# One query slot computed head by head, the first exponentials taken earlier, and four row batches mixed one step sooner in a two-layer PEER kernel

## The chip, the cores and the metric

The kernel runs on one core of a Trainium2 chip. The metric is the device time of one execution in microseconds (us); smaller is better. TensorE (PE) multiplies, ScalarE (ACT) and VectorE (DVE) work on vectors, GpSimd (POOL) issues the gathers of table rows, and SyncE (SP) issues the loads of weights.

## What is computed

The program runs two transformer layers and then a hybrid mixer and a mixture of experts. The change touches one part of each of the two layers, the PEER feed-forward:

```python
def peer_ffn(h, w_q, sub_keys, u_tab, v_tab):     # T = 256 tokens, 8 heads
    q = (xt @ w_q).reshape(T, PEER_HEADS, 2, PEER_HALF)
    s = jnp.einsum('thpd,hpnd->thpn', q, sub_keys)          # 16 blocks of 128 scores
    sv, si = lax.top_k(s, 16)
    cand = sv[:, :, 0, :, None] + sv[:, :, 1, None, :]
    cv, ci = lax.top_k(cand.reshape(T, PEER_HEADS, 256), 16)
    eidx = i1 * PEER_NKEYS + i2                             # 16 rows for a token and head
    gates = softmax(cv)
    ...
    act = gelu(einsum('cd,ckd->ck', xc, u_tab[ic]))
    return einsum('ck,ckd->cd', gc * act, v_tab[ic])
```

All of it is float32.

## The kernel before

The 256 tokens are two tiles of 128. A pair is one head of one tile, so there are 16 pairs, and each picks 16 rows for every token: 256 "rows" in a layer. One row here is one gather of 128 table rows of 2048 words (u and v side by side), 1 MB. `PICKS` is 256, and pairs 0 to 7 belong to tile 0.

The query matrix comes in four slots of 2 MB, with two heads (four blocks) each. `ring` holds two slots. SP loads a slot when the one two places before it has been used, which it sees by the semaphore `tile_done`; behind the four query slots it loads two slots of the gate matrix in the same way, and, when slot 3 is done, `proj_w` and `pT` (1 MB and 0.25 MB).

- Slot 0 (`first_heads`) is computed for tile 0, all four blocks, then for tile 1: query matmuls (L582), small matmuls that turn two pieces of a conditioning vector each (L528), and the score matmuls with the keys (L592). ACT takes each result out of PSUM (L1085, L1087).
- Slots 1 to 3 (`features`, L463, for both tiles at once, in four groups of matmuls j = 0 to 3) give queries that ACT evicts (L1092). Then come the score matmuls (L613) and their evictions (L1102).
- DVE's `topk(p)` finds the rows of pair p: its last instruction (L1538) releases `rows_ready`, and POOL then issues 16 gathers (L2010). The gathers have `ROWS` = 12 buffers, so gather n waits until row n - 12 has been mixed (`v_done`).
- DVE's loop over pairs takes the dot product of each row with the token (L1598). Between the dots it does one step of `topk(p + 2)`; the first step of `topk(2)` stands behind the dot of row 0 and waits for the scores of slot 1.
- For each batch of four rows ACT's `batch(at)` computes the gelu (L1074), DVE the gate (L1609), and ACT four diagonal matrices (L1080). PE's `mix_rows` (L566) then multiplies each diagonal with the v half of the row, adds into PSUM and releases `v_done`.
- `exponents(p)` (L1067) are the softmax exponentials of pair p. DVE's loop can't begin pair p without them.

PE works in program order. Between the query slots it mixes batch 0 halfway through slot 2, batch 4 behind slot 2's scores, and batch 8 halfway through slot 3; from row 12 on it mixes behind slot 3. ACT's order is written out by hand too: `exponents(0)` behind the second eviction of slot 1, `batch(0)` and `batch(4)` behind the first of slot 2, `batch(8)` behind the scores of slot 2, `batch(12)` behind the first eviction of slot 3.

Of the kernel before, what the change touches and what calls it, by code (L numbers as in the profile page):

```python
# [14 lines left out]
P = 128  # L15
T = 256
TT = T // P
# [4 lines left out]
PH = 8  # L22
# [12 lines left out]
PICKS = PAIRS * TOPK  # L35
BATCH = 4
# [7 lines left out]
    ("a_x", 2, "AA"), ("a_gates", 1, "A" * 8), ("a_y", 2, "AA"), ("a_out", 2, "DD"),  # L44
    ("peer_q0", 4, "AAAA"),
    ("ple_gate0", 2, "A"),
    ("qkv", 6, "AA"), ("bo", 2, "DD"),
    ("peer_q1", 4, "AAAA"),
    ("ple_gate1", 2, "A"),
    ("mix_in", 7, ("AA", "DD", "AA", "AA", "AA", "AA", "DD")), ("mix_out", 2, "DD"),  # L50
)
MIX = (4, 3, 5, 1, 0, 2, 6)
GATES = (0, 1, 2, 4, 5, 6, 3, 7)
CAP = 64
# [57 lines left out]
def build(nc, d):  # L112
# [7 lines left out]
    with ExitStack() as ctx:  # L120
# [321 lines left out]
        def _(pe):  # L442
# [111 lines left out]
            def peer(l, i):  # L554
# [16 lines left out]
                def first_heads():  # L571

                    n = FIRST[f"peer_q{l}"]
                    w = slot_in(n).rearrange("p (k f) -> p k f", k=KC)
                    m = ENDS[n] - 4
                    turn(i, h)
                    for t in range(TT):
                        pe.wait_ge(xT_ready, 4 * i + 4 * l + 2 * t + 2)
                        bank_free(m + 2 * t)
                        for f in range(4):  # L580
                            for k in range(KC):
                                mm = pe.matmul(psum[:, (m + 2 * t) % 3, f * P:(f + 1) * P], w[:, k, f * P:(f + 1) * P],  # L582
                                               xT[:, k, t * P:(t + 1) * P], start=(k == 0), stop=(k == KC - 1))
                        mm.then_inc(tile_done, 1)
                        for s in range(2 * t, 2 * t + 2):
                            turn_condition(8 * l + s)
                        if t == 0:
                            pe.wait_ge(keys_loaded, 16 * (l + 1))
                        pe.wait_ge(act_took, TILE_NTH[m + 2 * t])
                        bank_free(m + 2 * t + 1)  # L590
                        for f in range(4):
                            mm = pe.matmul(psum[:, (m + 2 * t + 1) % 3, f * P:(f + 1) * P], qT[:, f, t * P:(t + 1) * P],  # L592
                                           keys[:, f * NK:(f + 1) * NK], start=True, stop=True)
                        mm.then_inc(tile_done, 1)
# [6 lines left out]

                def half_way(at):
                    return lambda j: mix_early(at) if j == 1 else None

                for s in range(1, 4):
                    features(f"peer_q{l}", s, xT, between=half_way(8 * s - 16) if s >= 2 else None)
# [27 lines left out]

                for n in range(3 * BATCH, PICKS):
                    if n == 148:
# [369 lines left out]
        def _(act):  # L1006
# [54 lines left out]
            def peer(l, i):  # L1061
# [21 lines left out]
                m = tile0(f"peer_q{l}")  # L1083
                for t in range(TT):
                    act.activation(qT[:, 0:4, t * P:(t + 1) * P], tile_in(m + 2 * t).rearrange("p (a b) -> p a b", a=4),  # L1085
                                   ACT.Copy).then_inc(act_took, 1)
                    act.activation(scores[:, t, 0:4, :], tile_in(m + 2 * t + 1).rearrange("p (a b) -> p a b", a=4),  # L1087
                                   ACT.Copy).then_inc(act_took, 1)
                for s in range(1, 4):
                    m = tile0(f"peer_q{l}") + 4 * s  # L1090
# [220 lines left out]
        def _(dve):  # L1311
# [165 lines left out]
            def peer(l, i):  # L1477
# [19 lines left out]
                def topk(p):  # L1497

                    m = tile0(f"peer_q{l}") + 4 * (p % PH // 2)
                    dve.wait_ge(act_took, TILE_NTH[m + 2 + p // PH if p % PH // 2 else m + 1 + 2 * (p // PH)])  # L1500
                    for half in range(2):
# [592 lines left out]
```

## Time and profile before

| | us |
|---|---|
| median of 3 runs | 2948.27 |
| lowest and highest | 2947.35 and 2952.21 |
| the profiled execution | 2960.54 |
| its span, first to last instruction | 2958.7 |
| PE busy, share of the span | 89% |
| DVE, ACT, POOL busy | 46%, 21%, 17% |
| read from memory | 1047.69 MB |

The span is what the profile's time axis covers; 1.8 us of the profiled execution lie around it. That execution took 12.3 us more than the median of the runs without a profile. Times in the text count from the first instruction. A float32 matmul shows as two records, so four mixed rows (eight matmuls) are 16 records. The PEER part of layer 0 runs from about 108 to 822 us, that of layer 1 from about 995 to 1710 us.

### The profile page before, as it was taken

How to read it: one execution, taken by the hardware profiler on the slowest of the kernel's cores; microseconds unless marked ns; L12 is line 12 of the kernel's file. 1: busy time of each engine (PE TensorE's matmuls, PEld its weight loads, DVE VectorE, ACT ScalarE, POOL GpSimd, SP SyncE). 2: the span in 40 equal slices, each digit the busy share in tenths (PEclk: the TensorE clock that was granted, in tenths of full speed). 3: DMA queues.
4: the chain of work that ended last, by engine and by line, in shares of the span. 5: the costliest groups of instructions: out<-in, count | busy, mean ns of one | idle time of the engine just before them, and what ended most of it. 6: DMA issues, size and time to landing. Idle time of an engine off the chain costs nothing.

```text
span 2958.7 us, 28660 instructions
## 1 busy us (share of the span) xinstructions
PE 2623.4 (89%) x9706; PEld 1223.0 (41%) x9706; DVE 1368.7 (46%) x3391; ACT 616.2 (21%) x1232; POOL 489.4 (17%) x526
## 2 busy tenths in 40 slices
PE   8998787887799998787888799889999999999998
PEld 7663333333366663333333366543333232333333
DVE  5657777776425656777776541431111111111111
ACT  3022212232115122222232120211111111111111
POOL 0124333333200124333333200000000000000000
PEclk9999999999999999999999999889999999999999
DMA  5699999999863699999999833447999999899997
GB/s 217 264 377 422 421 421 421 421 420 421 347 240 143 249 377 422 421 421 421 421 421 421 345 127 114 180 199 321 422 422 422 422 422 422 352 422 422 376 400 295
DMA packets 145293, 1049.90 MB, mean 355 GB/s; under 512 B 16272, under 2 KB 16528, under 8 KB 17968
## 3 DMA queue, kind: packets, MB, share of 16 engines
q0 software_dynamic: 74064, 537.56, 43.8%
q1 hardware_dynamic: 70560, 509.12, 42.2%
q10 hardware_dynamic: 576, 2.13, 0.2%
q8 instruction: 41, 0.67, 0.1%
q14 instruction: 52, 0.43, 0.0%
HBM read 1047.69 MB, written 1.05 MB: 354 GB/s over the span
## 4 chain that ended last, share of the span: by engine, by line
PE 54%; DMA 37%; DVE 4%; ACT 2%; issue 1%; another core or an unknown queue 1%; DVEq 1%; SPq 0%; POOLq 0%
PE psum L566 14%; DMA big<-in_moe 13%; DMA uv_more<-in_peer_uv,rows_of 13%; DMA big<-in_peer_uv,rows_of 11%; PE psum L971 11%; PE psum L463 7%; PE psum L997 5%; PE psum L478 5%; PE psum L883 1%; PE psum L952 1%; PE psum L665 1%; PE psum L582 1%; DVE big L1598 1%; DVE uv_more L1598 1%; PE psum L965 1%
## 5 line engine op out<-in xcount | busy, mean ns | idle before, releaser
L566 PE MATMUL psum<-big,gdiag 128*128 128x512 f32 x1880 | 912.7, 642 | 233.1 <-ACT gdiag L1080 233.1
L1598 DVE CUSTOM_DVE_ANT_0 big<-psum,big 128x1024 f32<-128x1024 f32 x470 | 574.4, 1224 | 281.4 <-DMA big<-in_peer_uv,rows_of 274.8
L566 PEld LDWEIGHTS psum<-big,gdiag 128*128 128x128 f32 x1880 | 375.6, 205 | 761.9 <-issue 440.8
L2010 POOL DMA_INDIRECT big<-in_peer_uv,rows_of x470 | 444.7, 946 | 1158.2 <-PE psum L566 779.5
L971 PE MATMUL psum<-big 128*64 128x512 f32 x2240 | 500.9, 596 | 24.4 <-POOLq L2032 23.9
L1976 DVE TENSOR_SCALAR big<-psum 128x512 f32<-128x512 f32 x35 | 24.2, 692 | 667.5 <-PE psum L971 667.5
L971 PEld LDWEIGHTS psum<-big 128*64 128x64 f32 x2240 | 152.8, 137 | 370.7 <-issue 275.1
L997 PE MATMUL psum<-ring,big 128*64 128x512 f32 x1120 | 248.1, 594 | 3.8
L463 PE MATMUL psum<-big,ring 128*128 128x256 f32 x1088 | 241.2, 381 | 0.8 <-DVE big L1362 0.8
L463 PEld LDWEIGHTS psum<-big,ring 128*128 128x128 f32 x1088 | 206.5, 191 | 33.2 <-issue 3.8
L1074 ACT ACTIVATE gelu<-dots,rstd 128x4 f32<-128x4 f32 x128 | 38.0, 297 | 869.1 <-DVE dots L1598 869.1
L1080 ACT ACTIVATE gdiag<-small,gated 128x128 f32<-128x128 f32 x512 | 163.6, 390 | 49.8 <-DVE gated L1609 49.2
L478 PE MATMUL psum<-ring,big 128*128 128x512 f32 x352 | 156.3, 602 | 2.7 <-DVE big L1439 1.4
L997 PEld LDWEIGHTS psum<-ring,big 128*64 128x64 f32 x1120 | 92.5, 137 | 136.8 <-issue 132.1
L1294 ACT ACTIVATE big<-big 128x512 f32<-128x512 f32 x35 | 22.0, 630 | 489.3 <-DVE big L1976 489.3
L478 PEld LDWEIGHTS psum<-ring,big 128*128 128x128 f32 x352 | 66.8, 192 | 84.6 <-issue 79.7
L566 PE MATMUL psum<-uv_more,gdiag 128*128 128x512 f32 x168 | 78.9, 592 | 0.0
L952 PE MATMUL psum<-big 64*128 64x512 f32 x288 | 71.5, 615 | 0.7 <-ACT big L1302 0.7
L883 PE MATMUL psum<-big 128*64 128x512 f32 x288 | 71.3, 617 | 0.0
L1302 ACT ACTIVATE big<-psum 128x512 f32<-128x512 f32 x35 | 20.9, 597 | 231.0 <-PE psum L997 231.0
L1609 DVE SCALAR_TENSOR_TENSOR gated<-gelu,gsum,gexp 128x4 f32<-128x4 f32 x128 | 28.1, 219 | 81.7 <-ACT gelu L1074 79.2
L1598 DVE CUSTOM_DVE_ANT_0 uv_more<-psum,uv_more 128x1024 f32<-128x1024 f32 x42 | 51.4, 1224 | 24.8 <-DMA uv_more<-in_peer_uv,rows_of 24.2
(385 smaller groups left out, 1969.2 us busy)
## 6 DMA issues: line engine op xcount, KB each, us to landing
big<-in_moe SPq DMA_DIRECT2D x256, 1024.0 KB, 20.7
ring<-in_moe SPq DMA_DIRECT2D x128, 1024.0 KB, 19.4
big<-in_ada SPq DMA_DIRECT2D x24, 1024.0 KB, 11.8
ring<-in_peer_wq SPq DMA_DIRECT2D x16, 1024.0 KB
ring<-in_mix_in SPq DMA_DIRECT2D x14, 1024.0 KB
ring<-in_a_in SPq DMA_DIRECT2D x8, 1024.0 KB
ring<-in_ple_gate SPq DMA_DIRECT2D x8, 1024.0 KB
ring<-in_kv SPq DMA_DIRECT2D x8, 1024.0 KB
```

What stands on the lines that cost most here:

```text
L463: mm = pe.matmul(psum[:, (m + t) % 3, f * T:(f + 1) * T], w[:, k, c:c + P], rhs[:, k, :], start=(k == 0), stop=(k == KC - 1))
L478: mm = pe.matmul(psum[:, (m + t) % 3, :], lhs[:, k, t * P:(t + 1) * P], w[:, k, :], start=(k == 0), stop=(k == KC - 1))
L566: mm = pe.matmul(psum[:, OUT_BANK[t] + c, :], gdiag[:, n % DIAGS, :], uv[(PICKS * l + n) % ROWS][:, D + c * 512:D + (c + 1) * 512], start= ...
L582: mm = pe.matmul(psum[:, (m + 2 * t) % 3, f * P:(f + 1) * P], w[:, k, f * P:(f + 1) * P], xT[:, k, t * P:(t + 1) * P], start=(k == 0), sto ...
L883: mm = pe.matmul(psum[CAP * c:CAP * (c + 1), 2, :], S[:, t, :], hs[:, t, c * 512:(c + 1) * 512], start=(t == 0), stop=(t == TT - 1), skip_ ...
L952: mm = pe.matmul(psum[:, 4 + 2 * t + c, :], SGT[r, t * P:(t + 1) * P], Y[r, :], start=False, stop=stop, skip_group_check=True)
L971: mm = pe.matmul(psum[CAP * c:CAP * (c + 1), b, :], xgT[:, k % 4, k // 4, :], wring[k][:, (2 * b + c) * 512:(2 * b + c + 1) * 512], start= ...
L997: mm = pe.matmul(psum[CAP * c:CAP * (c + 1), 2, :], actT[:, j, f * CAP:(f + 1) * CAP], wring[8 + j][:, (2 * f + c) * 512:(2 * f + c + 1) * ...
L1074: act.activation(gelu[:, cols], dots[:, cols], ACT.Gelu_apprx_tanh, scale=rstd[:, t:t + 1]).then_inc(gelu_ready, 1)
L1080: act.activation(gdiag[:, n % DIAGS, :], ident, ACT.Copy, scale=gated[:, n:n + 1]).then_inc(gdiag_ready, 1)
L1598: j = dve.tensor_tensor_reduce(out=u, in0=x, in1=u, scale=1.0, scalar=0.0, op0=ALU.mult, op1=ALU.add, accum_out=dots[:, n:n + 1])
L2010: pool.indirect_dma_start(uv[g % ROWS], None, table, bass.IndirectOffsetOnAxis(rows_of[:, n:n + 1], 0)).then_inc(uv_loaded[g % ROWS], 16)
```

## The change

Three parts. (1) Slot 0 is computed in three parts instead of two: head 0 of tile 0, head 1 of tile 0, then both heads of tile 1 (`FIRST_HEADS`), each with its own queries, evictions and scores; `topk(0)` and `topk(1)` wait for their own head's scores alone. The four turns of the conditioning vector are spread as one, one, two. (2) ACT takes `exponents(0)` right behind the evictions of slot 0, and `batch(0)` behind slot 1's scores and `exponents(1)`. (3) PE mixes batch 0 behind the first group of slot 2 (of four), batch 4 behind its third, batch 8 behind slot 2's scores, and batch 12 halfway through slot 3; behind slot 3 it goes on with row 16.

```diff
-    ("peer_q0", 4, "AAAA"),
+    ("peer_q0", 4, ("AAAAAA", "AAAA", "AAAA", "AAAA")),
...
+FIRST_HEADS = ((0, (0, 1)), (0, (2, 3)), (1, (0, 1, 2, 3)))
...
-                    for t in range(TT):
+                    for part, (t, blocks) in enumerate(FIRST_HEADS):
                         pe.wait_ge(xT_ready, 4 * i + 4 * l + 2 * t + 2)
-                        bank_free(m + 2 * t)
-                        for f in range(4):
+                        q, s = m + 2 * part, m + 2 * part + 1
+                        bank_free(q)
+                        for j, f in enumerate(blocks):
...
-                        for s in range(2 * t, 2 * t + 2):
-                            turn_condition(8 * l + s)
+                        for c in ((0,), (1,), (2, 3))[part]:
+                            turn_condition(8 * l + c)
...
-                def half_way(at):
-                    return lambda j: mix_early(at) if j == 1 else None
+                inside = {2: {0: 0, 2: BATCH}, 3: {1: 3 * BATCH}}
+
+                def mix_inside(s):
+                    return lambda j: mix_early(inside[s][j]) if j in inside[s] else None
...
                     if s == 2:
-                        mix_early(BATCH)
+                        mix_early(2 * BATCH)
...
-                for n in range(3 * BATCH, PICKS):
+                for n in range(4 * BATCH, PICKS):
...
+                exponents(0)
                 for s in range(1, 4):
...
-                        if s == 1 and g == 1:
-                            exponents(0)
                         if s == 2 and g == 0:
-                            batch(0)
                             batch(4)
...
                     if s == 1:
                         exponents(1)
+                        batch(0)
...
-                    dve.wait_ge(act_took, TILE_NTH[m + 2 + p // PH if p % PH // 2 else m + 1 + 2 * (p // PH)])
+                    dve.wait_ge(act_took, TILE_NTH[m + 2 + p // PH if p % PH >= 2 else
+                                                   tile0(f"peer_q{l}") + (5 if p >= PH else 1 + 2 * p)])
```

On ACT, this stands before the change from the first eviction of slot 1 on (`gdiag` are the diagonals, `gexp` the exponentials):

```order
L1092 ACTIVATE big<-psum 128x512 [waits tile_done] x2
L1067 ACT_TABLE_LOAD
L1067 ACTIVATE gexp<-gexp,rstd 128x16 [waits gexp_in]
L1102 ACTIVATE big<-psum 128x512 [waits tile_done] x2
L1067 ACTIVATE gexp<-gexp,rstd 128x16 [waits gexp_in]
L1092 ACTIVATE big<-psum 128x512 [waits tile_done]
L1074 ACT_TABLE_LOAD
L1074 ACTIVATE gelu<-dots,rstd 128x4 [waits dots_ready]
L1080 ACTIVATE gdiag<-small,gated 128x128 [waits gated_act]
L1080 ACTIVATE gdiag<-small,gated 128x128 x3
```

And this stands there after it, from the last eviction of slot 0 on:

```order
L1093 ACTIVATE big<-psum 128x512 [waits tile_done]
L1071 ACT_TABLE_LOAD
L1071 ACTIVATE gexp<-gexp,rstd 128x16 [waits gexp_in]
L1100 ACTIVATE big<-psum 128x512 [waits tile_done] x2
L1107 ACTIVATE big<-psum 128x512 [waits tile_done] x2
L1071 ACTIVATE gexp<-gexp,rstd 128x16 [waits gexp_in]
L1078 ACT_TABLE_LOAD
L1078 ACTIVATE gelu<-dots,rstd 128x4 [waits dots_ready]
L1084 ACTIVATE gdiag<-small,gated 128x128 [waits gated_act]
L1084 ACTIVATE gdiag<-small,gated 128x128 x3
L1100 ACTIVATE big<-psum 128x512 [waits tile_done]
```

The first exponential has moved ahead of slot 1's evictions, and the first gelu with its diagonals ahead of slot 2's first eviction; the number of table loads is the same.

On PE, slot 2 begins like this before the change (L463 is the slot's queries, L566 the mixing of a row, two matmuls each):

```order
L463 MATMUL psum<-big,ring 128x256 [waits act_took,half_loaded3,half_loaded2]
L463 MATMUL psum<-big,ring 128x256 x15
L566 MATMUL psum<-big,gdiag 128x512 [waits gdiag_ready]
L566 MATMUL psum<-big,gdiag 128x512
L566 MATMUL psum<-big,gdiag 128x512 [waits gdiag_ready]
L566 MATMUL psum<-big,gdiag 128x512
L566 MATMUL psum<-big,gdiag 128x512 [waits gdiag_ready]
L566 MATMUL psum<-big,gdiag 128x512
L566 MATMUL psum<-big,gdiag 128x512 [waits gdiag_ready]
L566 MATMUL psum<-big,gdiag 128x512
L463 MATMUL psum<-big,ring 128x256 [waits act_took]
L463 MATMUL psum<-big,ring 128x256 x15
```

And like this after it:

```order
L464 MATMUL psum<-big,ring 128x256 [waits act_took,half_loaded3,half_loaded2]
L464 MATMUL psum<-big,ring 128x256 x7
L567 MATMUL psum<-big,gdiag 128x512 [waits gdiag_ready]
L567 MATMUL psum<-big,gdiag 128x512
L567 MATMUL psum<-big,gdiag 128x512 [waits gdiag_ready]
L567 MATMUL psum<-big,gdiag 128x512
L567 MATMUL psum<-big,gdiag 128x512 [waits gdiag_ready]
L567 MATMUL psum<-big,gdiag 128x512
L567 MATMUL psum<-big,gdiag 128x512 [waits gdiag_ready]
L567 MATMUL psum<-big,gdiag 128x512
L464 MATMUL psum<-big,ring 128x256 x8
L464 MATMUL psum<-big,ring 128x256 [waits act_took]
```

Batch 0 stands eight matmuls earlier in slot 2. Batch 4, formerly behind slot 2's scores, follows eight matmuls before the slot's last ones, and so on for the next two.

## Rows read from the trace of the kernel before

**Rows 1.** The page: memory traffic in 40 equal slices, and the chain by engine.

```profile
GB/s 217 264 377 422 421 421 421 421 420 421 347 240 143 249 377 422 421 421 421 421 421 421 345 127 114 180 199 321 422 422 422 422 422 422 352 422 422 376 400 295
...
PE 54%; DMA 37%; DVE 4%; ACT 2%; issue 1%; another core or an unknown queue 1%; DVEq 1%; SPq 0%; POOLq 0%
```

**Rows 2.** Windows: PE, PEld, DVE, ACT, POOL busy, granted clock, DMA share, GB/s.

```profile
130.00:215.00 85.00, 75.06 (x304) 55.23 (x303) 45.27 (x141) 18.62 (x40) 22.88 (x24) 0.94 0.94 375
215.00:800.00 585.00, 475.62 (x998) 197.84 (x996) 410.78 (x1030) 138.78 (x340) 219.28 (x232) 0.93 1.01 421
1018.00:1105.00 87.00, 77.21 (x306) 55.91 (x305) 46.21 (x143) 20.61 (x44) 23.50 (x25) 0.94 0.94 378
1105.00:1300.00 195.00, 154.75 (x321) 63.86 (x320) 138.98 (x361) 44.44 (x111) 75.76 (x80) 0.93 1.01 422
```

**Rows 3.** The same view, two windows in which the DMA traffic begins.

```profile
130.00:135.00 5.00, 5.00 (x27) 4.46 (x26) 4.33 (x22) 0.31 (x1) 2.88 (x3) 1.00 0.85 288
...
1015.00:1020.00 5.00, 5.00 (x37) 4.77 (x37) 4.19 (x18) 0.74 (x2) 0.94 (x1) 1.00 0.32 72
```

**Rows 4.** Timeline of DVE, layer 0: start us, us, what, [idle before it <- releaser].

```profile
113.33 5.70 DVE L1451 SCALAR_TENSOR_TENSOR big<-big,cond 128x512 f32<-128x512 f32 x7
120.51 0.29 DVE L1487 MAX8 sv<-big 128x8 f32<-128x128 f32 x1 [1.47 <-ACT big L1087]
...
130.39 0.18 DVE L1538 SCALAR_TENSOR_TENSOR rows_of<-picked 128x16 uint32<-128x16 f32 x1
```

**Rows 5.** Timelines of the issuing engines SP and POOL, layer 0.

```profile
213.19 0.43 SPq L384 DMA_DIRECT2D big<-in_ple_proj  x1
...
131.52 1.14 POOL L2010 DMA_INDIRECT big<-in_peer_uv,rows_of  x1 [131.07 <-DVE rows_of L1538]
...
145.57 0.94 POOL L2010 DMA_INDIRECT uv_more<-in_peer_uv,rows_of  x1 [0.31 <-issue]
```

**Rows 6.** Timeline of PE, layer 0.

```profile
130.38 13.98 PE L463 MATMUL psum<-big,ring 128*128 128x256 f32 x64
149.26 3.78 PE L613 MATMUL psum<-keys,big 128*128 128x128 f32 x16 [4.90 <-ACT big L1092]
152.84 7.73 PE L463 MATMUL psum<-big,ring 128*128 128x256 f32 x32
163.55 8.83 PE L566 MATMUL psum<-big,gdiag 128*128 128x512 f32 x16 [2.99 <-ACT gdiag L1080]
...
181.86 7.03 PE L566 MATMUL psum<-big,gdiag 128*128 128x512 f32 x16
...
210.26 2.05 PE L613 MATMUL psum<-keys,big 128*128 128x128 f32 x16 [0.69 <-ACT big L1092]
```

**Rows 7.** Timeline of ACT, layer 0.

```profile
148.61 0.60 ACT L1092 ACTIVATE big<-psum 128x512 f32<-128x512 f32 x1 [10.52 <-remote]
...
151.37 0.60 ACT L1102 ACTIVATE big<-psum 128x512 f32<-128x512 f32 x1 [0.55 <-PE psum L613]
...
195.84 0.60 ACT L1092 ACTIVATE big<-psum 128x512 f32<-128x512 f32 x1 [11.43 <-PE psum L463]
...
196.91 1.28 ACT L1080 ACTIVATE gdiag<-small,gated 128x128 f32<-128x128 f32 x4 [0.29 <-DVE gated L1609]
```

**Rows 8.** Timeline of DVE, layer 0: first step of topk(2), dot of row 3.

```profile
152.39 0.29 DVE L1487 MAX8 sv<-big 128x8 f32<-128x128 f32 x1
...
157.49 1.23 DVE L1598 CUSTOM_DVE_ANT_0 big<-psum,big 128x1024 f32<-128x1024 f32 x1
```

**Rows 9.** Timelines of PE and ACT, layer 1.

```profile
1050.96 8.83 PE L566 MATMUL psum<-big,gdiag 128*128 128x512 f32 x16 [2.99 <-ACT gdiag L1080]
...
1099.76 0.60 ACT L1102 ACTIVATE big<-psum 128x512 f32<-128x512 f32 x1 [0.30 <-PE psum L613]
1100.37 1.28 ACT L1067 ACT_TABLE_LOAD   x1
...
1103.88 1.28 ACT L1080 ACTIVATE gdiag<-small,gated 128x128 f32<-128x128 f32 x4 [0.29 <-DVE gated L1609]
```

More of the change, by code:

```diff
@@ L44 @@
     ("a_x", 2, "AA"), ("a_gates", 1, "A" * 8), ("a_y", 2, "AA"), ("a_out", 2, "DD"),
-    ("peer_q0", 4, "AAAA"),
+    ("peer_q0", 4, ("AAAAAA", "AAAA", "AAAA", "AAAA")),
     ("ple_gate0", 2, "A"),
     ("qkv", 6, "AA"), ("bo", 2, "DD"),
-    ("peer_q1", 4, "AAAA"),
+    ("peer_q1", 4, ("AAAAAA", "AAAA", "AAAA", "AAAA")),
     ("ple_gate1", 2, "A"),
@@ L574, in first_heads @@
                     w = slot_in(n).rearrange("p (k f) -> p k f", k=KC)
-                    m = ENDS[n] - 4
+                    m = ENDS[n] - 6
                     turn(i, h)
-                    for t in range(TT):
+                    for part, (t, blocks) in enumerate(FIRST_HEADS):
                         pe.wait_ge(xT_ready, 4 * i + 4 * l + 2 * t + 2)
-                        bank_free(m + 2 * t)
-                        for f in range(4):
+                        q, s = m + 2 * part, m + 2 * part + 1
+                        bank_free(q)
+                        for j, f in enumerate(blocks):
                             for k in range(KC):
-                                mm = pe.matmul(psum[:, (m + 2 * t) % 3, f * P:(f + 1) * P], w[:, k, f * P:(f + 1) * P],
+                                mm = pe.matmul(psum[:, q % 3, j * P:(j + 1) * P], w[:, k, f * P:(f + 1) * P],
                                                xT[:, k, t * P:(t + 1) * P], start=(k == 0), stop=(k == KC - 1))
                         mm.then_inc(tile_done, 1)
-                        for s in range(2 * t, 2 * t + 2):
-                            turn_condition(8 * l + s)
-                        if t == 0:
+                        for c in ((0,), (1,), (2, 3))[part]:
+                            turn_condition(8 * l + c)
+                        if part == 0:
                             pe.wait_ge(keys_loaded, 16 * (l + 1))
[L589 to L592, printed above, removed]
+                        pe.wait_ge(act_took, TILE_NTH[q])
+                        bank_free(s)
+                        for j, f in enumerate(blocks):
+                            mm = pe.matmul(psum[:, s % 3, j * P:(j + 1) * P], qT[:, f, t * P:(t + 1) * P],
                                            keys[:, f * NK:(f + 1) * NK], start=True, stop=True)
@@ L600, in mix_early @@
                         mix_rows(n)
-                def half_way(at):
-                    return lambda j: mix_early(at) if j == 1 else None
+                inside = {2: {0: 0, 2: BATCH}, 3: {1: 3 * BATCH}}
+                def mix_inside(s):
+                    return lambda j: mix_early(inside[s][j]) if j in inside[s] else None
                 for s in range(1, 4):
-                    features(f"peer_q{l}", s, xT, between=half_way(8 * s - 16) if s >= 2 else None)
+                    features(f"peer_q{l}", s, xT, between=mix_inside(s) if s in inside else None)
                     m = ENDS[FIRST[f"peer_q{l}"] + s] - 2
@@ L1083, in peer @@
                 m = tile0(f"peer_q{l}")
-                for t in range(TT):
-                    act.activation(qT[:, 0:4, t * P:(t + 1) * P], tile_in(m + 2 * t).rearrange("p (a b) -> p a b", a=4),
+                for part, (t, blocks) in enumerate(FIRST_HEADS):
+                    f, n = slice(blocks[0], blocks[-1] + 1), len(blocks)
+                    act.activation(qT[:, f, t * P:(t + 1) * P],
+                                   tile_in(m + 2 * part)[:, 0:n * P].rearrange("p (a b) -> p a b", a=n),
                                    ACT.Copy).then_inc(act_took, 1)
-                    act.activation(scores[:, t, 0:4, :], tile_in(m + 2 * t + 1).rearrange("p (a b) -> p a b", a=4),
+                    act.activation(scores[:, t, f, :],
+                                   tile_in(m + 2 * part + 1)[:, 0:n * P].rearrange("p (a b) -> p a b", a=n),
                                    ACT.Copy).then_inc(act_took, 1)
+                exponents(0)
                 for s in range(1, 4):
-                    m = tile0(f"peer_q{l}") + 4 * s
+                    m = tile0(f"peer_q{l}") + 4 * s + 2
                     for g in range(2):
@@ L1497, in topk @@
                 def topk(p):
-                    m = tile0(f"peer_q{l}") + 4 * (p % PH // 2)
-                    dve.wait_ge(act_took, TILE_NTH[m + 2 + p // PH if p % PH // 2 else m + 1 + 2 * (p // PH)])
+                    m = tile0(f"peer_q{l}") + 4 * (p % PH // 2) + 2
+                    dve.wait_ge(act_took, TILE_NTH[m + 2 + p // PH if p % PH >= 2 else
+                                                   tile0(f"peer_q{l}") + (5 if p >= PH else 1 + 2 * p)])
                     for half in range(2):
```

## The prediction

> **What bounds the kernel now.** I began with the page. Its traffic row stands at 420 to 422 GB/s for most of two stretches, slices 4 to 10 and 16 to 22: these are the gathers of the two PEER parts, and the chain gives DMA 37% of the span [rows 1]. So I cut windows. From 215 to 800 us the DMA engines carry 421 GB/s, from 1105 to 1300 us 422 [rows 2]: there nothing but the amount of data counts. The stretch ahead of each is where time can be had: 375 GB/s from 130 to 215 us and 378 from 1018 to 1105 us [rows 2]. Against 421 that is 85 x (1 - 375/421) = 9.3 us and 87 x (1 - 378/421) = 8.9 us of empty DMA. Part of it is the ramp: 288 GB/s in 130 to 135 us means data from 131.6 us on, and 72 GB/s in 1015 to 1020 us data from 1019.1 us on [rows 3]. What is left, 7.7 and 7.8 us, is starvation in the query slots, and it is all that the change can win there. A layer's gathers end when the DMA has moved all its bytes, so a us of starvation saved or added is a us of the kernel, in each layer. One row is 1.049 MB, at 421 GB/s 2.49 us.
>
> **Part 1, slot 0 by heads.** It removes and adds no matmul: 32 + 32 query matmuls become 16 + 16 + 32. PE should reach slot 1 at the same 130.4 us [rows 6]; the eviction between queries and scores stays behind the turn of the conditioning vector. ACT has two evictions more in a layer, in idle time. `topk(0)` began at 120.51 us after DVE had waited 1.47 us for its scores; before that DVE was busy with the sums until 113.33 + 5.70 = 119.03 us [rows 4]. Head 0's scores have 32 records of 128 columns less ahead of them; 64 records of 256 columns take 13.98 us [rows 6], so these are 3.5 us, and the scores come at 117 us at the latest. DVE is now the limit, and `topk(0)`, with its first rows at 130.39 us [rows 4] and POOL's first gather at 131.52 us [rows 5], comes 1.45 us earlier. I price these 1.45 us at nothing: data flow from 131.6 us already, hardly after POOL's first issue, because SP has issued the weights of slot 2 when slot 0 was done. Earlier gathers change the order of bytes that are moved without a gap: rows 0 to 15 and slots 2 and 3 are 20 rows' worth, enough until 131.6 + 20 x 2.49 = 181.4 us.
>
> The Trainium skill (DMA: Bandwidth & Descriptors, Queues, rings and completion order) says that a DMA engine goes round between the queues that have work, packet by packet. By that the gathers would only take a share of slot 2's bandwidth sooner, which is again nothing in the sum.
>
> **Part 2, exponentials and batch 0.** DVE's loop no longer waits for `exponents(0)`, so the dot of row 0 can be taken sooner, by about the 10.5 us that ACT stood still ahead of 148.61 us [rows 7]. But behind it stands the first step of `topk(2)`, which waits for slot 1's scores, evicted at 151.37 + 0.60 = 151.97 us [rows 7]. That step began at 152.39 us [rows 8]. It gains 0.4 us, and the dot of row 3, which ended at 157.49 + 1.23 = 158.7 us [rows 8], ends at 158.3 us. The gain lies behind that: ACT has no eviction ahead of the gelu any more. From the start of an eviction to the start of the diagonals are 196.91 - 195.84 = 1.07 us, of which 0.5 is the eviction, and the first of four diagonals takes 0.32 us [rows 7]. So the first diagonal is ready at about 159.3 us. Before, batch 0 began on PE at 163.55 us after a wait of 2.99 us [rows 6].
>
> **Part 3, the mixing in the slots.** In slot 2 the first group of queries ends at about 156.9 us, about half of the 32 records that took 7.73 us from 152.84 us on [rows 6]. PE then waits 2.4 us for the diagonal instead of 2.99. Batch 4 needs nothing new. Batch 8 now stands right behind slot 2's scores, but its gelu stands on ACT behind the evictions of these scores; batch 12 stands right behind the half slot whose eviction ACT takes before that gelu. Either time PE waits for eviction, gelu, gate and first diagonal: 1.07 + 0.32 = 1.4 us from the eviction's start [rows 7], 1.45 with the semaphore. Before the change, batches 4 and 8 found their diagonals ready (181.86 us follows the scores without a wait [rows 6]).
>
> What this does to the DMA is a balance of two things. Four rows more are mixed ahead of slot 3's end, so four gathers more, 4 x 2.49 = 9.96 us of data, are to be had before the last weights come. And slot 3 ends later, with the loads behind it (second gate slot, projection), issued 0.9 us after its scores (210.26 + 2.05 = 212.31, and 213.19 us [rows 5, 6]). It ends later by 6.87 us for four rows (7.03 us of records that overlap [rows 6]), plus 2 x 1.45 us for the new waits, less 0.6 us for the shorter one: 9.2 us. So the starvation falls by 0.8 us only. If the stretch at half clock does not come again that made batch 0 take 8.83 us where batch 4 took 7.03 [rows 6, 9], slot 3 ends 1.8 us less late, 7.4 us, and 2.6 us are saved. I take the middle, 1.7 us, since the wait ahead of batch 0 is only a little shorter than the one that had it. The granted clock's mean was 0.94 in both stretches [rows 2]. The same rows hold in layer 1, where batch 0 waited 2.99 us and took 8.83 us too [rows 9].
>
> The Trainium skill (TensorE: Matmul & The Clock Gate, Part 1) says that the array's usual state is the throttled one and that only activity releases it. Taken as it stands it speaks against the change, which adds two gaps; with batch 0 slow as before, its sum is 0.8 us a layer and 2946.7 us.
>
> **Behind slot 3** PE now meets row 16 at once, and row 16's gelu waits for the scores' evictions, a table load, an exponential and another table load. In layer 1 the second eviction began at 1099.76 us and the diagonals at 1103.88 us [rows 9], so the first is ready 4.5 us after the scores, and row 28 can be gathered 1.8 us later, 6.3 us after the scores. Gate slot, `proj_w` and `pT` are 3.25 rows' worth, 8.1 us of data from an issue at 0.9 us: work until 9.0 us in these terms. The new stall on PE is covered by 2.7 us, less if gathers take longer from issue to data than weights; without cover it costs its own length.
>
> **Sum.** The profiled execution (2960.54 us, of which 2958.7 are span) would lose 2 x 1.7 = 3.4 us. It stands 12.3 us over the median of the runs, and I carry the difference over: 2948.3 - 3.4 = 2945 us. Below 0.2%, 5.9 us, a measurement of this kernel can't tell a change from none.
>
> **Rivals.** *The pause behind slot 1 shortens.* PE's last record of slot 1 ends at 144.36 us, yet ACT is released at 148.61 us by something that the view calls remote [rows 6, 7]; that is 2.1 us after POOL's last issue of the first twelve ends at 146.51 us [rows 5]. PE then ran its scores in 3.78 us instead of 2.05, and 32 records of slot 2 in 7.73 instead of 13.98 / 2 = 7.0 us [rows 6]. I can't name the cause. If it is tied to POOL's train, which now ends 1.45 us sooner, slot 3 ends 1.5 to 2 us sooner: 3 to 4 us more, 2941 us. If it goes, 4.25 us with the 1.7 and 0.7 us of slow matmuls go, more than the 6.0 us of starvation left in each layer: 2933 us. Chance 0.25 for both, mostly the first.
>
> *The timed runs have no such pause.* Their 12.3 us less than the profiled one speak for it. Then slot 3 ended at about 205.6 us before (212.31 less 4.25, 1.7 and 0.7), 30 rows' worth of data (24 rows, slots 2 and 3 and a gate slot) lasted to 131.6 + 74.7 = 206.3 us, and there was hardly any starvation to save. The new slot 3 ends 6.87 + 2.9 + 0.5 = 10.3 us later against 9.96 us of data: 0.3 to 1 us slower in each layer, 2949 us. Chance 0.2.
>
> *The earlier start counts in full.* 2 x 1.45 us more: 2942 us. It would need an empty DMA until POOL's gathers come, and [rows 3] speak against it. Chance 0.05.
>
> *Slower: half clock in the slots.* If the two new waits each bring a stretch at half clock like that behind the 2.99 us wait, 1.8 us each, slot 3 ends 9.2 + 3.6 = 12.8 us later against 9.96 us of data: 2.8 us lost in each layer, 2954 us. It decides from 9.96 us of delay on, and from 12.9 us on it is slower by 0.2%. That the 0.69 us waits at the scores bring nothing speaks against it; that the new ones are twice as long, for it. Chance 0.12.
>
> **How the numbers follow.** My forecast, 0.8 to 2.6 us saved in each layer with a us or two of slack either way, 2942 to 2948 us, has 0.38. Faster by over 0.2% means under 2942.4: most of the first rival, half of the third, and a tail of the forecast, 0.27. Slower means over 2954.2: half of the fourth and what I have not seen, 0.13. The rest, 0.60, is no difference. The range from 2937 to 2954 us leaves out 0.2: the case in which the pause goes, and what lies beyond the slow clock.
>
> **What would show it.** `topk(0)` starts at about 119.05 us with no wait for ACT; the first gather at about 130.1 us, with the data's start unmoved. The dot of row 0 comes near 141 us and that of row 1 only behind 152 us. Batch 0 is mixed from about 159.4 us, with waits of some 1.4 us ahead of batches 8 and 12. Slot 3's scores end at 219.7 to 221.5 us, row 16 starts 4.5 us later. The traffic has no gap any more behind 181.4 us, its last one has moved from before 213 us to before 222 us, and 130 to 215 us carry more than 375 GB/s. The forecast is wrong if slot 3 ends outside these limits, if ACT's pause at 138 to 148.6 us changes, or if a gap opens behind row 28.

## The result

The changed kernel takes 2955.55 us (median of 22 runs), the kernel before 2947.93 us (22 runs beside it): ratio 1.0022, interval 1.0012 to 1.0031. The change costs 7.6 us. Two later comparisons give 1.0019 (1.0006 to 1.0033) and 1.0023 (1.0011 to 1.0035). The profiled execution of the changed kernel spans 2953.1 us.

The page of the changed kernel, traffic and chain, beside [rows 1]:

```profile
GB/s 217 254 402 406 421 421 421 421 421 422 353 229 141 246 410 414 421 422 421 421 422 421 345 127 116 179 198 328 422 422 422 421 422 422 350 422 422 379 401 295
...
PE 55%; DMA 35%; DVE 5%; ACT 2%; issue 1%; DVEq 1%; SPq 0%; POOLq 0%
```

Slices 3 and 15 carry more than before (402 for 377, 410 for 377), slices 4 and 16 less (406 for 422, 414 for 421). The gap has not gone, it has moved behind 215 us. The windows of the changed kernel (columns as in [rows 2]), first the four stretches of [rows 2], then the end of slot 3 in layer 0 piece by piece and that part of either layer as a whole:

```profile
130.00:215.00 85.00, 76.60 (x298) 53.20 (x298) 45.55 (x142) 15.00 (x34) 26.45 (x28) 0.96 0.98 401
215.00:800.00 585.00, 475.98 (x1020) 200.48 (x1018) 410.25 (x1030) 142.57 (x345) 214.18 (x228) 0.93 1.01 417
1018.00:1105.00 87.00, 77.90 (x312) 54.85 (x311) 44.91 (x139) 15.66 (x36) 26.30 (x28) 0.98 0.99 409
1105.00:1300.00 195.00, 155.90 (x336) 65.29 (x334) 142.09 (x371) 49.88 (x120) 74.09 (x79) 0.93 1.00 414
...
215.00:220.00 5.00, 4.31 (x27) 3.68 (x26) 0.00 (x0) 1.18 (x2) 0.00 (x0) 1.00 0.78 324
220.00:225.00 5.00, 1.48 (x12) 1.06 (x10) 0.83 (x2) 4.35 (x8) 0.00 (x0) 0.87 0.73 244
225.00:230.00 5.00, 5.00 (x6) 2.05 (x7) 4.63 (x12) 0.71 (x3) 0.94 (x1) 0.50 0.99 417
230.00:235.00 5.00, 5.00 (x12) 2.23 (x11) 4.67 (x16) 1.57 (x5) 1.87 (x2) 0.95 0.93 317
235.00:240.00 5.00, 5.00 (x13) 2.28 (x12) 4.69 (x11) 0.00 (x0) 2.81 (x3) 1.00 1.01 375
205.00:245.00 40.00, 35.80 (x110) 19.66 (x109) 25.37 (x67) 9.39 (x21) 12.17 (x13) 0.91 0.93 357
1075.00:1135.00 60.00, 53.55 (x168) 30.07 (x167) 33.43 (x92) 14.94 (x35) 18.45 (x20) 0.97 0.98 397
```

There are two gaps, one ahead of the gate weights (324 and 244 GB/s) and one behind row 28's gather (317 and 375 GB/s); another 1.0 us is missing between 205 and 215 us (378 and 382 GB/s). Against 421 GB/s the last two rows are 40 x (1 - 357/421) = 6.1 us and 60 x (1 - 397/421) = 3.4 us of empty DMA.

PE in layer 0 (start us, us, what, [idle before it]):

```profile
132.24 13.98 PE L464 MATMUL psum<-big,ring 128*128 128x256 f32 x64
146.90 2.05 PE L617 MATMUL psum<-keys,big 128*128 128x128 f32 x16 [0.69 <-ACT big L1100]
148.79 3.62 PE L464 MATMUL psum<-big,ring 128*128 128x256 f32 x16
156.32 10.05 PE L567 MATMUL psum<-big,gdiag 128*128 128x512 f32 x16 [3.91 <-ACT gdiag L1084]
...
187.90 5.42 PE L567 MATMUL psum<-big,gdiag 128*128 128x512 f32 x12 [1.56 <-ACT gdiag L1084]
...
203.50 7.13 PE L567 MATMUL psum<-big,gdiag 128*128 128x512 f32 x16 [1.56 <-ACT gdiag L1084]
...
218.23 2.05 PE L617 MATMUL psum<-keys,big 128*128 128x128 f32 x16 [0.69 <-ACT big L1100]
...
224.89 15.05 PE L567 MATMUL psum<-big,gdiag 128*128 128x512 f32 x28 [2.83 <-ACT gdiag L1084]
```

The reader is to see four waits for diagonals, and behind two of them mixing that is slow: 10.05 us for 16 records that take 7.03 us at the full clock, and 15.05 us for 28 that take 12.2 us. The window 225 to 230 us shows the granted clock at 0.50, the lower of the two levels (1.2 GHz), and the one behind the first wait 0.54:

```profile
155.00:160.00 5.00, 3.68 (x5) 1.61 (x6) 4.67 (x17) 1.58 (x5) 0.00 (x0) 0.54 1.01 423
```

DVE, POOL and ACT of the same execution, their timelines one after the other:

```profile
120.82 0.28 DVE L1493 MAX8 sv<-big 128x8 f32<-128x128 f32 x1
...
130.69 0.18 DVE L1545 SCALAR_TENSOR_TENSOR rows_of<-picked 128x16 uint32<-128x16 f32 x1
...
132.70 1.14 POOL L2017 DMA_INDIRECT big<-in_peer_uv,rows_of  x1 [132.25 <-PE psum L559]
...
210.91 0.94 POOL L2017 DMA_INDIRECT big<-in_peer_uv,rows_of  x1 [0.78 <-PE psum L567]
228.94 0.94 POOL L2017 DMA_INDIRECT big<-in_peer_uv,rows_of  x1 [17.09 <-PE psum L567]
...
146.25 0.60 ACT L1100 ACTIVATE big<-psum 128x512 f32<-128x512 f32 x1 [6.31 <-PE psum L464]
...
155.11 0.30 ACT L1078 ACTIVATE gelu<-dots,rstd 128x4 f32<-128x4 f32 x1 [4.02 <-DVE dots L1605]
```

`topk(0)` no longer waits for ACT, and its rows come 1.6 us sooner, counted from the start of slot 0's queries (130.69 - 111.61 = 19.1 us for 130.39 - 109.75 = 20.6 us before). But POOL's first gather is released by PE (the conditioning vector, L559), not by DVE. POOL stands still for 17.09 us from row 27 to row 28. And ACT's eviction at 146.25 us follows PE at once: the pause of [rows 7] is not in this execution.

### The profile page after: what moved, and what is told of

It reads as the page before. It is cut to its first block, busy times and chain, and to the rows that moved or that the text cites. A ratio compares the mean times of both kernels' runs of the same rounds, so it can differ in the third digit from the quotient of the medians.

```text
span 2953.1 us, 28668 instructions
## 1 busy us (share of the span) xinstructions
PE 2624.6 (89%) x9706; PEld 1220.8 (41%) x9706; DVE 1367.5 (46%) x3391; ACT 616.7 (21%) x1236; POOL 486.5 (16%) x526
## 4 chain that ended last, share of the span: by engine, by line
PE 55%; DMA 35%; DVE 5%; ACT 2%; issue 1%; DVEq 1%; SPq 0%; POOLq 0%
PE psum L567 15%; DMA big<-in_moe 13%; DMA big<-in_peer_uv,rows_of 12%; PE psum L975 11%; DMA uv_more<-in_peer_uv,rows_of 10%; PE psum L464 7%; PE psum L1001 5%; PE psum L479 5%; PE psum L887 1%; DVE big L1605 1%; PE psum L956 1%; PE psum L669 1%; PE psum L584 1%; PE psum L969 1%; PE psum L629 1%
```

## The experiments

Sixteen runs in four series of four; a series shares its runs of the kernel before. Times are medians with the ratio to the kernel before, timed beside it, and its 95% interval. "Slot 3" below is the start of its scores, less the start of slot 0's queries, since that start lies at 109.3 to 109.8 us in some executions and at 111.3 to 112.0 us in others, whatever the kernel.

### The kernel before again, and the parts

**e1_before_again**, the kernel before unchanged.

> The kernel before, unchanged. Theory A (the pause of 4.2 us behind slot 1 belongs to that one profiled execution, and the timed runs have none): ratio 1.000, and a new profile may come without the pause; then its span is about 2946 us instead of 2958.7, slot 3's scores end some 6.5 us earlier than 212.3 us and 130 to 215 us carry about 400 GB/s. Rival B (the pause is a part of this program): it stands there again in both layers, with a span near 2958.7 us.

Measured: 2948.01 us, 1.0002 (0.999 to 1.0015), span 2941.8 us. Its profile has no pause.

**e2_early_exp**, parts 1 and 2 with the order of mixing of before:

```diff
-inside = {2: {0: 0, 2: BATCH}, 3: {1: 3 * BATCH}}
+inside = {2: {1: 0}, 3: {1: 2 * BATCH}}
...
-                        mix_early(2 * BATCH)
+                        mix_early(BATCH)
...
-                for n in range(4 * BATCH, PICKS):
+                for n in range(3 * BATCH, PICKS):
```

> Parts 1 and 2 of the change (slot 0 by heads, exponents(0) and batch(0) early on ACT) with the mixing order of the kernel before. Theory A (the loss comes from the mixing order, which ends slot 3 later and exposes row 16): no loss, 0 to 3 us faster than before (ratio 0.999 to 1.000), slot 3's scores end at or before the time they end without a pause, about 205 us. Rival C (the loss comes from the heads or from the early exponentials): it stays slower, ratio near 1.002.

Measured: 2946.68 us, 0.9996 (0.9987 to 1.0005). Batch 0 waits 0.46 us and takes 7.13 us; slot 3 is 89.7 us; 205 to 245 and 1075 to 1135 us both carry 421 GB/s, so the DMA is full where it was empty for 1.3 us in each layer of e1. It is not full further on in layer 0. The same window of e2 and of e1, in that order:

```profile
560.00:610.00 50.00, 49.04 (x115) 21.55 (x114) 35.06 (x93) 17.28 (x35) 18.88 (x21) 1.00 0.99 399
560.00:610.00 50.00, 47.71 (x112) 20.83 (x111) 36.17 (x98) 17.28 (x35) 18.53 (x20) 1.00 1.01 421
```

That is 50 x (1 - 399/421) = 2.6 us of empty DMA, as much as the two layers have gained.

**e3_no_heads**, parts 2 and 3 with slot 0 as before (`peer_q0` and `peer_q1` "AAAA", the two-tile loop in slot 0):

> Parts 2 and 3 of the change (early exponentials and batch 0, mixing one step sooner) with slot 0 as before. Theory A: as slow as the change, ratio 1.002 to 1.003. Rival C1 (the loss comes from slot 0 by heads): as fast as before, 1.000.

Measured: 2954.33 us, 1.0021 (1.001 to 1.0032); slot 3 106.7 us. Without part 1 the loss is the same.

**e4_three_batches**, the change with twelve rows ahead of slot 3's end:

```diff
-inside = {2: {0: 0, 2: BATCH}, 3: {1: 3 * BATCH}}
+inside = {2: {0: 0, 2: BATCH}, 3: {1: 2 * BATCH}}
...
-                    if s == 2:
-                        mix_early(2 * BATCH)
...
-                for n in range(4 * BATCH, PICKS):
+                for n in range(3 * BATCH, PICKS):
```

> The change, but only three batches are mixed ahead of slot 3's end as in the kernel before: batch 0 and batch 4 inside slot 2 as in the change, batch 8 halfway through slot 3, nothing behind slot 2's scores, and row 12 first behind slot 3. Theory A: slot 3's scores end 8 to 9 us earlier than in the change (220.3 us less 111.61 - 109.75 for the later start of layer 0's part), the DMA traffic has no gap behind row 28, and the loss is gone: ratio 0.999 to 1.001. Rival C (heads or early exponentials): near 1.002.

Measured: 2953.17 us, 1.0012 (1.0002 to 1.0023). PE in layer 0 and the two windows of this kernel:

```profile
156.06 10.11 PE L567 MATMUL psum<-big,gdiag 128*128 128x512 f32 x16 [3.91 <-ACT gdiag L1082]
...
207.50 2.05 PE L617 MATMUL psum<-keys,big 128*128 128x128 f32 x16 [0.69 <-ACT big L1098]
```

```profile
205.00:245.00 40.00, 35.13 (x102) 17.15 (x101) 23.03 (x58) 12.55 (x28) 15.45 (x16) 0.99 0.95 388
1075.00:1135.00 60.00, 53.95 (x160) 28.71 (x159) 35.70 (x99) 15.90 (x35) 20.82 (x22) 0.97 0.97 399
```

It mixes as many rows ahead of slot 3's end as the kernel before, batches 0 and 4 eight matmuls earlier, and has slot 3 at 96.2 us for 94.0: the early mixing alone delays slot 3 by 2.2 us, and more of the DMA is empty (3.1 + 3.1 us) than in e16 below. The expected 0.999 to 1.001, no loss without the four rows, was missed: part of the loss is there without them. What the four rows do by themselves is seen in e14 below.

### Undoing one piece of part 3

**e5_row16_early** and **e6_batch0_later** each undo one, **e7_later_and_row16** both, **e8_heads_only** is part 1 alone. The edit of e5, on ACT, in slot 3 and in the loop behind it:

```diff
                         if s == 3 and g == 0:
                             batch(12)
+                            exponents(2)
+                            batch(16)
...
-                        if at >= 16:
+                        if at >= 20:
                             batch(at)
...
-                    if p + 2 < PAIRS:
+                    if 0 < p < PAIRS - 2:
                         exponents(p + 2)
```

The edit of e6, on PE (batch 0 where it was, batches 4 and 8 behind slot 2's scores):

```diff
-inside = {2: {0: 0, 2: BATCH}, 3: {1: 3 * BATCH}}
+inside = {2: {1: 0}, 3: {1: 3 * BATCH}}
...
                     if s == 2:
+                        mix_early(BATCH)
                         mix_early(2 * BATCH)
```

> The changed kernel with one move: the exponential of the third pair and the gelu and diagonals of rows 16 to 19 stand on ACT right behind batch 12, ahead of the evictions of slot 3's second group of queries and of its scores. Theory (two gaps: slot 3 ends too late, and row 16's stall of 2.83 us with half clock behind it makes row 28's gather late): PE's row 16 follows the scores of slot 3 with no wait and at the full clock, the traffic between 230 and 240 us rises from 317 and 375 GB/s to 420, which is 1.8 us, and in layer 1 about 0.9 us; the gap before 225 us stays. Time 2.7 us under the change, ratio to the kernel before 1.0013. Rival one (the whole loss is slot 3's late end): the ratio stays at 1.0022. Rival two (the exponential or the dots of rows 16 to 19 are not ready in slot 3, ACT waits for DVE and slot 3's scores come later still): slower than the change, 1.003.

> The changed kernel with batch 0 mixed where the kernel before mixes it, between the two groups of slot 2, and batches 4 and 8 both behind slot 2's scores; batch 12 halfway slot 3, so still 16 rows ahead of slot 3's end. Theory (it is the waits and the half clock of the early batch 0, not the number of rows): PE waits about 0.5 us ahead of batch 0 and takes 7.1 us for it, the 1.56 us wait ahead of batch 8 goes, slot 3's scores come near 210 us instead of 218.2, which is less than four rows' 9.96 us of data behind the 203.4 us of the kernel before, so the gap before 225 us goes; ratio 1.0000 to 1.0005. Rival (the number of rows mixed ahead of slot 3's end costs, or the stall of row 16 does): scores near 210 us all the same, but the gap moves behind them, ratio 1.0015 or more.

> The moves of the two runs above together. Theory: no gap in the traffic from 135 to 245 us nor in layer 1, as in the kernel that had the order of mixing of before with the early exponentials; ratio 0.9990 to 0.9998. Rival (sixteen rows ahead of slot 3's end always cost): 1.001 or more.

> The kernel before with part 1 alone: slot 0's queries by heads for tile 0, the exponentials, batch 0 and the order of mixing as before. Theory (DVE is bound by its sums, POOL by the vector turned behind slot 1's start, and the DMA is full from 132 us on): the first exponential rows of topk come earlier and nothing else, ratio 0.9995 to 1.0005. Rival one (the earlier start counts): 0.999. Rival two (it costs, by the matmuls at half clock at the start of slot 0 or the two evictions more): 1.001.

Measured: e5 2956.98 us, 0.9995 (0.9985 to 1.0005); e6 2949.19 us, 0.9972 (0.996 to 0.9983); e7 2944.36 us, 0.9952 (0.9937 to 0.9967, six runs); e8 2954.17 us, 0.9991 (0.9978 to 1.0005). But the kernel before took 2956.48 us (28 runs) beside them, 8.6 us more than in the first series, and all four profiles have the pause. ACT and PE of e5 in layer 0:

```profile
149.56 0.60 ACT L1100 ACTIVATE big<-psum 128x512 f32<-128x512 f32 x1 [9.89 <-remote]
```

```profile
150.21 3.78 PE L617 MATMUL psum<-keys,big 128*128 128x128 f32 x16 [4.27 <-ACT big L1100]
153.78 4.36 PE L464 MATMUL psum<-big,ring 128*128 128x256 f32 x16
160.55 7.13 PE L567 MATMUL psum<-big,gdiag 128*128 128x512 f32 x16 [2.40 <-ACT gdiag L1084]
...
219.55 2.05 PE L617 MATMUL psum<-keys,big 128*128 128x128 f32 x16 [0.69 <-ACT big L1100]
```

The same wait as in [rows 7], for all kernels of the series. Under it batch 0 behaves as forecast (a wait of 2.40 us in layer 0, 2.26 us in layer 1), since the slow scores and queries give the diagonals time. All four ratios lie under what was expected; those numbers were made for a series without the pause, and three of the four kernels were timed again without it below.

### The same again, and the pause

**e9_after_again**, **e10_before_again2**, **e11_early_exp_again**, **e12_later_and_row16_again** are the change, the kernel before, e2 and e7, unchanged.

> The changed kernel unchanged, run again beside e10. Two theories of what decides its worth. Theory A (the pause decides): the pause of about 4 us on ACT and PE behind slot 1's queries is there for all kernels of one series of runs or for none; in a series without it the kernel before takes 2948 us and has hardly any starvation to lose, so the change costs 0.2% (ratio 1.0022, as measured); in a series with it the kernel before takes 2956 us with 7.7 us of starvation a layer, slot 3 of the change ends 3 to 4 us later than in its own trace too, and the ratio is 0.998 to 1.0005, 2951 to 2958 us. Theory B (the change costs in any state): ratio 1.002 in either, so 2962 us with the pause.

> The kernel before, for its profile in this series. Theory A: its median is 2947 to 2949 us if its profile has no pause (scores of slot 1 at about 144.7 us) and 2955 to 2958 us if it has it (scores at about 149 us), never the one with the other. Rival: pause and median are not tied to each other. Ratio 1.0000.

> The kernel with parts 1 and 2 alone and the order of mixing of before, again. In a series without the pause 0.9990 to 1.0000, as before (0.9996). In a series with it: batch 0 meets its diagonals with hardly a wait, so 2.5 us of wait and 1.7 us of half clock go in each layer, all of it out of starvation: 0.9970 to 0.9975. Rival (parts 1 and 2 are worth nothing with the pause either, the wait only moves to another place): 1.000.

> Sixteen rows mixed ahead of slot 3's end, but batch 0 halfway slot 2 and rows 16 to 19 ready ahead of slot 3's end, again. In a series without the pause slot 3's scores come near 208 us, data last, no gap: 0.9985 to 0.9995, within the interval of e11. In a series with it 0.995 as before. Rival (0.9952 was a matter of its six runs): 0.998 or more with the pause.

Measured: e9 2953.42 us, 1.0019 (1.0006 to 1.0033); e10 2945.73 us, 0.9992 (0.9981 to 1.0003); e11 2947.99 us, 1.0 (0.9988 to 1.0012); e12 2948.07 us, 1.0001 (0.9991 to 1.0011), beside 2947.97 us of the kernel before. None of the four profiles has the pause. e7 and e12 are one kernel: 0.9952 beside the pause (six runs), 1.0001 without it, where 0.9985 to 0.9995 was expected. Theory A keeps its first half (pause and 2956 us of the kernel before go together, no pause and 2946 to 2948 us too); its second half, what the change is worth under the pause, had no run here.

**e13_row16_early_again**, **e14_batch0_later_again**, **e15_after_third** and **e16_before_third** are e5, e6, the change and the kernel before.

> Rows 16 to 19 made ready inside slot 3, the rest as the change. Without the pause: the gap behind row 28 (230 to 240 us and layer 1, together 2.7 us) goes, the one ahead of 225 us stays, ratio 1.0010 to 1.0015. If row 16's stall is the whole cause 1.0000, if it is none of it 1.002. With the pause 0.9995 as in e5.

> Batch 0 halfway slot 2 and batches 4 and 8 both behind slot 2's scores, row 16's stall left as in the change. Without the pause: slot 3's scores near 212 us instead of 218.2, 5 us of the late end undone, only row 16's gap stays, ratio 1.0005 to 1.0010. If the early batch 0 is none of the cause 1.002. With the pause 0.997 as in e6.

> The changed kernel. Without the pause 1.002 for the third time. With the pause (the condition of the profile on which the prediction was made) theory A says 0.998 to 1.0005, theory B 1.002.

> The kernel before, for its profile: with the pause of slot 1 its median is 2955 to 2958 us, without it 2946 to 2949 us. Ratio 1.0000.

Measured, again without the pause: e13 2949.33 us, 1.0014 (1.0003 to 1.0025); e14 2945.97 us, 0.9999 (0.9989 to 1.001); e15 2954.06 us, 1.0023 (1.0011 to 1.0035); e16 2945.86 us, 1.0002 (0.999 to 1.0013). ACT, PE and two windows of e16, the kernel before:

```profile
146.61 0.60 ACT L1092 ACTIVATE big<-psum 128x512 f32<-128x512 f32 x1 [6.31 <-PE psum L463]
```

```profile
147.26 2.05 PE L613 MATMUL psum<-keys,big 128*128 128x128 f32 x16 [0.69 <-ACT big L1092]
149.15 7.07 PE L463 MATMUL psum<-big,ring 128*128 128x256 f32 x32
159.21 8.83 PE L566 MATMUL psum<-big,gdiag 128*128 128x512 f32 x16 [2.99 <-ACT gdiag L1080]
...
205.92 2.05 PE L613 MATMUL psum<-keys,big 128*128 128x128 f32 x16 [0.69 <-ACT big L1092]
```

```profile
205.00:245.00 40.00, 35.02 (x95) 16.31 (x94) 24.37 (x61) 13.84 (x29) 15.36 (x17) 0.96 0.99 407
1075.00:1135.00 60.00, 50.79 (x151) 26.14 (x150) 37.76 (x104) 15.42 (x34) 22.21 (x24) 1.00 1.00 412
```

Slot 3 is 94.0 us here, for 100.5 us under the pause ([rows 6], started at 109.75 us), and the DMA is empty for 1.3 us in each layer. PE and windows of e14, where batch 0 stands halfway slot 2 and sixteen rows are mixed ahead of slot 3's end:

```profile
156.43 7.13 PE L567 MATMUL psum<-big,gdiag 128*128 128x512 f32 x16 [0.46 <-ACT gdiag L1085]
...
173.05 12.18 PE L567 MATMUL psum<-big,gdiag 128*128 128x512 f32 x28
...
210.15 2.05 PE L617 MATMUL psum<-keys,big 128*128 128x128 f32 x16 [0.69 <-ACT big L1101]
...
216.81 14.24 PE L567 MATMUL psum<-big,gdiag 128*128 128x512 f32 x28 [2.82 <-ACT gdiag L1085]
```

```profile
205.00:245.00 40.00, 34.71 (x103) 17.71 (x102) 24.14 (x61) 13.84 (x29) 12.35 (x14) 0.96 1.01 421
1075.00:1135.00 60.00, 49.61 (x148) 25.91 (x146) 36.56 (x104) 16.69 (x38) 18.85 (x20) 0.97 1.01 421
```

Slot 3 is 98.4 us: 4.5 us later than in e16, for 9.96 us of data more. The stall of row 16 is still there (2.82 us, then slow mixing), and the traffic has no gap behind it: data last. The expected 1.0005 to 1.0010, with a gap there, was missed on the good side. From 560 to 610 us e14 carries 399 GB/s, like e2. In e13, which keeps the early batch 0, row 16's stall is gone and slot 3 is 105.2 us; its first gap remains:

```profile
215.00:220.00 5.00, 4.31 (x28) 3.40 (x29) 3.70 (x12) 2.65 (x7) 0.00 (x0) 1.00 0.65 218
...
205.00:245.00 40.00, 37.75 (x122) 20.73 (x121) 27.37 (x75) 10.85 (x26) 14.95 (x17) 1.00 0.97 396
```

The ratios without the pause, by the place of batch 0 and the rows mixed ahead of slot 3's end:

| | 12 rows | 16 rows |
|---|---|---|
| batch 0 halfway slot 2 | 0.9996, 1.0 (e2, e11) | 0.9999 (e14) |
| batch 0 behind slot 2's first group | 1.0012 (e4) | 1.0022, 1.0019, 1.0023 (the change, e9, e15) |

So the mixing in slot 2 moved ahead is the cause: undone, it gives all of the loss back (1.0023 to 0.9999, intervals just apart), with the four rows kept. The edit moves batch 4 too, which then stands ahead of batch 8 and takes away the wait of 1.56 us there. Of 105.2 - 98.4 = 6.8 us in layer 0 (e15 against e14), the shorter wait for batch 0 is 3.5 us, its faster records 1.5 us (8.62 to 7.13), and that wait 1.6 us; no run moves batch 0 alone. Row 16's stall undone gives back 0.0009, which the intervals (1.0011 to 1.0035 and 1.0003 to 1.0025) don't tell from nothing; that it costs only because the early batch has used up the data that cover it is read from the two traces.

## Why the prediction was wrong

It said 2945 us (2937 to 2954); 2955.55 us were measured. Two steps failed, and both rest on the pause of the one profiled execution. The first is "What is left, 7.7 and 7.8 us, is starvation in the query slots, and it is all that the change can win there". That starvation came with the pause. In all three later profiles of the kernel before the pause is absent and 1.0 to 1.3 us (407 or 408, and 412 or 414 GB/s) are empty in each layer, so there was next to nothing to win. The prediction carried the 12.3 us between the profiled execution and the median over as if they lay outside the stretch; 8.6 us is what the kernel before differs by between the series with the pause and the first without it.

This takes the gain away, but makes no loss. The loss comes from the second, the balance of part 3: "PE then waits 2.4 us for the diagonal instead of 2.99" and with it a slot 3 that ends 7.4 to 9.2 us later, under the 9.96 us of data that four rows bring. It ended 12.7 us later in layer 0 and 11.2 us in layer 1, and the stall behind it was not covered. The excess is 12.7 - 9.96 = 2.7 us and the stall costs 1.8 us, together 4.5 us, where the layer has 6.1 - 1.3 = 4.8 us more of empty DMA; in layer 1 1.3 and 0.9 us (396 and 369 GB/s in 1115 to 1125 us), 2.2 us for 3.4 - 1.3 = 2.1 us.

Point by point:

- **Part 1.** Priced at nothing, and nothing is seen of it (e3 against the change; e8 0.9991, its interval holds 1). `topk(0)` gains the forecast time (1.6 us for 1.45). The forecast of POOL's first gather at 130.1 us was wrong: it is held by the vector turned behind slot 0, which the prediction did not count.
- **Part 2.** Right in mechanism. With the order of before, batch 0's wait falls from 2.99 to 0.46 us and its half clock goes (e2); 1.2 us and 0 us faster (e2, e11) are both within their intervals of no change, though the DMA was full all the way in the slots and 2.6 us should be won. The traces show where they go: 2.6 us of DMA are empty from 560 to 610 us (399 GB/s in e2 and e14, 398 in e11, 403 in e12: the four profiles with full slots), where the kernel before carries 421, 417 and 417 GB/s. So "a us of starvation saved or added is a us of the kernel, in each layer" failed for what was saved in layer 0. What opens that gap is not shown.
- **Part 3, the delay of slot 3.** Forecast 7.4 to 9.2 us; measured in layer 0 against 93.96 us of the kernel before 11.2 us (e15, 105.20 us) to 12.7 us (the change, 106.62 us). The term "PE then waits 2.4 us for the diagonal instead of 2.99" was mis-sized: it is 3.91 us. The first diagonal comes about as forecast, 156.32 - 146.90 = 9.4 us behind the start of slot 1's scores (forecast 10.0); but the first group of queries is done 5.5 us behind it, not 7.6, since without the pause the scores take 2.05 us and the 16 query records 3.62 us. e5, under the pause, has 2.40 us in layer 0, and its slot 3 comes at 108.2 us for 100.5 us of the kernel before, 7.7 us later and within the forecast. The two new waits are 1.56 us (forecast 1.45) and 3.4 us together with what the records then overlap less. The sum is 0.9 for the wait, -0.2 to 1.3 for batch 0 (8.6 to 10.2 us for 8.83), 3.4, and 7.0 for four rows: 11.1 to 12.6 us.
- **Behind slot 3.** "The new stall on PE is covered by 2.7 us" failed: the mixing of row 16 and on runs slowly behind the stall (15.05 us for 28 records, 2.9 more than at the full clock), and POOL's row 28 starts 228.94 - (218.23 + 2.05) = 8.7 us behind slot 3's scores, not 6.3. The slower gathers cost 5 x (1 - 317/421) + 5 x (1 - 375/421) = 1.8 us in layer 0; e13 stands 0.0009, about 2.7 us, under e15 with it undone, though their intervals overlap.
- **The rivals.** "The timed runs have no such pause" was the right case, with 0.2: its "slot 3 ended at about 205.6 us" is what e1 shows (203.40 + 2.05 us). It was sized at 0.3 to 1 us a layer and 2949 us, since it took the short wait of 2.4 us along from the profile in which the pause stood, and full cover behind slot 3. "Half clock in the slots" had its sign right, but named the wrong waits: those of 1.56 us bring none (7.13 us behind one, 5.42 and 1.88 us behind the other), those of 2.8 and 3.9 us do. That its figures, 12.8 us later and 2954 us, lie next to 12.7 us and 2955.55 us is luck: it began at 9.2 us of delay and the pause, and counted 3.6 us for waits that cost no clock. The trace agrees here with the Trainium skill (TensorE: Matmul & The Clock Gate, Part 1) that the throttled state is what the array falls back to: granted clock 0.50 behind the 2.83 us.

Adding it up: the change leaves 6.1 + 3.4 us empty, the kernel before 1.3 + 1.3 us, 6.9 us more for 7.6 us in the time. The other two pairs of profiles give 9.1 us for 5.5 us (e9, e10) and 5.9 us for 7.9 us (e15, e16): one execution stands for its median only to some 4 us, and the three together, 7.3 us for 7.0 us, agree.

What stays open: what makes the pause (the trace calls its releaser remote, in both layers, at the same instruction in five kernels; the first series, without it, ran on the same chip as the second, with it, so the chip alone does not decide), what empties the DMA at 560 to 610 us, and what the change itself is worth under the pause. With one piece undone it stood at 0.9995 there (e5), at 1.0014 without it (e13).

## What to carry over

Profile the kernel before a second time before pricing a gain on a stall that only one execution shows, above all where the median of the runs is shorter than that execution by more than the gain. Look for a gain in the whole of the stretch that it should shorten: in e2 the 2.6 us won in the slots were lost again 350 us later. Work moved ahead of its inputs did not fill a gap here but opened one in front of everything behind it: PE waited 3.91 us for batch 0 in a place where it could have done 3.6 us of queries, and the mixing that followed ran slowly. The order with the early exponentials, batch 0 halfway slot 2 and sixteen rows ahead of slot 3's end (e7 and e12, 2944.36 and 2948.07 us) equals the kernel before without the pause and was 0.5% faster under it, in six runs of one series. That it is the data in reserve ahead of slot 3's end that cover the pause is an inference; no run tests it.

## What the runs showed of the hardware

- A pause of 3.5 to 4.2 us at one instruction, in both layers, came with a whole series of runs (PE's wait ahead of slot 1's scores is 4.2 to 4.9 us there, 0.69 us elsewhere): four kernels of the second series and the first profile of the kernel before have it, thirteen profiles of the others do not. The kernel before took 2956.48 us beside it and 2946.12 to 2947.97 us in the three series without it.
- In the query slots a wait of 1.57 us or less ahead of mixing, and e5's of 2.40 us, left 16 records at 7.13 us; waits of 2.99 to 3.92 us were followed by 8.6 to 10.2 us. Behind the slots the length of the wait did not decide alone: 8.83 us followed 2.02 us (the first profile of the kernel before, 1184.56 us), 7.13 us followed 2.80 us (e11, 441.79 us). The changed kernel's granted clock was 0.54 in 155 to 160 us and 0.50 in 225 to 230 us.
- The start of slot 0 lies about 2 us later in about half of the executions, with the same kernel (109.5 us in e10, 112.0 us in e16).
